# Rotary embedding of the "hg" mixers: from 32 partitions by 1024 columns in place to 128 partitions by 256 columns through gathered copies

## The reference, cut to what matters

```python
z = h @ w_in[l]                       # 256 x 8704: q, f, i, g, then q, k, v of attention, then two gates
qkv = zatt.reshape(B, S, 3, N_GROUPS, ATT_HEADS, ATT_DIM)     # 3 groups, 4 heads, 128 features
for g, (window, dilation) in enumerate(ATT_GROUPS):
    qg = partial_rope(qkv[:, :, 0, g], cos, sin)
    kg = partial_rope(qkv[:, :, 1, g], cos, sin)
    o_g, lse_g = dilated_window_attention(qg, kg, qkv[:, :, 2, g], window, dilation)
# partial_rope: of the 128 features of a head only the first 32 are rotated, as two halves of 16:
#   [r1 * cos - r2 * sin, r2 * cos + r1 * sin, rest unchanged]
```

## Time and profile before

| | |
|---|---|
| runs | 1879.37 us median of 3 (1879.2 to 1879.43) |
| profiled execution | 1879.31 us, of which 1877.5 us lie between its first and last instruction; mean granted clock of TensorE 0.999 |
| TensorE matmul busy | 1863.6 us (99%) |
| VectorE busy | 1265.3 us (67%) |
| ScalarE busy | 944.4 us (50%) |
| GpSimd busy | 62.9 us (3%) |
| DMA | 342.58 MB, mean 182 GB/s |

### The profile page before, as it was taken

One profiled execution on the slowest core, in us unless ns is written; L12 is line 12 of the kernel. 1 busy time (PEld: TensorE's weight loads), 2 busy tenths in 40 slices (PEclk: granted clock), 3 DMA queues, 4 the chain that ended last, 5 costly groups with the idle time before them and its releaser, 6 DMA issues.

```text
span 1877.5 us, 25275 instructions
## 1 busy us (share of the span) xinstructions
PE 1863.6 (99%) x9637; PEld 1586.2 (84%) x9637; DVE 1265.3 (67%) x1559; ACT 944.4 (50%) x1225; POOL 62.9 (3%) x94
## 2 busy tenths in 40 slices
PE   9999999999999999999999999999999999999998
PEld 7888988888888898888889888888889888888886
DVE  4466786466546668745576997677656797776754
ACT  5454574554345446445446545545444645445543
POOL 1010100000000000000000000000000000000000
PEclk9999999999999999999999999999999999999999
DMA  9667545656665665666555554455665554465562
GB/s 327 193 195 218 196 140 193 192 181 186 207 195 183 180 187 145 207 198 184 181 173 185 164 181 143 134 193 186 201 192 174 181 191 159 133 190 170 189 191 79
DMA packets 173656, 342.58 MB, mean 182 GB/s; under 512 B 10992, under 2 KB 11168, under 8 KB 173424
## 3 DMA queue, kind: packets, MB, share of 16 engines
q1 hardware_dynamic: 169376, 327.26, 56.1%
q0 software_dynamic: 4176, 13.90, 2.3%
HBM read 338.49 MB, written 1.05 MB: 181 GB/s over the span
## 4 chain that ended last, share of the span: by engine, by line
PE 88%; DVE 10%; issue 1%; ACT 1%; POOL 0%; POOLq 0%; DVEq 0%; ACTq 0%
PE stream L2365 18%; PE stream L2367 18%; PE stream L2366 18%; PE stream L2560 6%; PE stream L2561 3%; PE aux L2418 3%; DVE wlo L1313 3%; PE stream L2540 3%; PE stream L2541 3%; PE stream L2542 3%; PE stream L2403 2%; PE stream L2394 1%; PE stream L2395 1%; PE stream L2477 1%; PE stream L2479 1%; PE stream L2478 1%
## 5 line engine op out<-in xcount | busy, mean ns | idle before, releaser
L1313 DVE TENSOR_TENSOR wlo<-raw,whi 128x1024 fp32r<-128x1024 f32 x582 | 703.8, 1222 | 472.2 <-ACT whi L786 469.3
L786 ACT ACTIVATE whi<-raw 128x1024 fp32r<-128x1024 f32 x582 | 607.1, 1056 | 543.6 <-PE stream L2367 429.6
L2365 PE MATMUL stream<-whi,x_split 128*128 128x512 f32 x944 | 373.3, 395 | 1.5 <-DVE ak L1324 0.6
L2367 PE MATMUL stream<-whi,x_split 128*128 128x512 f32 x944 | 368.1, 390 | 0.0
L2366 PE MATMUL stream<-wlo,x_split 128*128 128x512 f32 x944 | 367.5, 389 | 0.0
L2365 PE MATMUL stream<-whi,hhi 128*128 128x512 f32 x672 | 263.3, 392 | 0.0
L2367 PE MATMUL stream<-whi,hlo 128*128 128x512 f32 x672 | 261.6, 389 | 0.0
L2366 PE MATMUL stream<-wlo,hhi 128*128 128x512 f32 x672 | 261.5, 389 | 0.0
L2560 PE MATMUL stream<-x_split,whi 128*128 128x512 f32 x672 | 241.4, 398 | 2.8 <-DVE ak L1324 2.1
L2367 PEld LDWEIGHTS stream<-whi,x_split 128*128 128x128 f32 x944 | 177.2, 188 | 37.9
L2365 PEld LDWEIGHTS stream<-whi,x_split 128*128 128x128 f32 x944 | 177.3, 188 | 37.3 <-DVE x_split L1349 1.5
(11 more groups left out here) (345 smaller groups left out, 2105.9 us busy)
## 6 DMA issues: line engine op xcount, KB each, us to landing
raw<-ffn_w_gu SPq DMA_DIRECT2D x175, 512.0 KB, 4.4
raw<-w_in SPq DMA_DIRECT2D x136, 512.0 KB, 4.6
raw<-ffn_w_down SPq DMA_DIRECT2D x88, 512.0 KB, 3.8
raw<-w_up SPq DMA_DIRECT2D x64, 512.0 KB, 4.4
raw<-w_down SPq DMA_DIRECT2D x64, 512.0 KB, 4.3
raw<-c_w_in SPq DMA_DIRECT2D x24, 512.0 KB, 3.9
raw<-ab_w_in SPq DMA_DIRECT2D x20, 512.0 KB, 4.9
raw<-w_out SPq DMA_DIRECT2D x16, 512.0 KB, 3.7
```

Source lines behind the costliest of these rows:

```text
L786: act.activation(split_slots(lin, at, j)[0], raw[:, b % RAW], ACT.Copy).then_inc(hi_ready, 1)
L1313: dve.tensor_tensor(lo, raw[:, b % RAW], hi.bitcast(F32), ALU.subtract).then_inc(lo_ready, 1)
L2365: pe.matmul(bank[tt][:], hi, wh, start=kt == 0, stop=False)
L2367: mm = pe.matmul(bank[tt][:], lo, wh, start=False, stop=kt == last)
```

## The change

The rotation of a chunk no longer works in place. GpSimd gathers the four heads below one another, 32 partitions each, into `rope_own` (the values) and `rope_swap` (the halves exchanged): per chunk eight transfers of 16 partitions by 256 tokens (16 KB) and four of 32 partitions (32 KB). VectorE rotates on 128 partitions by 256 columns. GpSimd then waits for that rotation and issues four transfers of 32 KB that put the rows back into `aq` or `ak`, with a semaphore of their own, `rope_out`; only then does it come to the next chunk. VectorE's rotation moves from the end of loop c (`use`) to the middle of loop c + 1, ahead of block 2's split. ScalarE's exponential of a level moves from the end of loop c to between the splits of blocks 0 and 1 of loop c + 1. TensorE waits for `rope_out` in place of `roped`. The tables of cos and sin are repeated over 128 partitions.

```diff
-    for tag, half, inv, width in (("a", 32, inv_a, P), ("b", 16, inv_b, 32)):
+    for tag, half, inv, width in (("a", 32, inv_a, P), ("b", 16, inv_b, P)):
...
-        rope_swap = [sb(f"rope_swap{i}", [32, 4, S], at=(86 + 4 * i) * KB) for i in range(2)]
+        rope_own = [sb(f"rope_own{i}", [P, S], at=(86 + 2 * i) * KB) for i in range(2)]
+        rope_swap = [sb(f"rope_swap{i}", [P, S], at=(87 + 2 * i) * KB) for i in range(2)]
...
                     pool.wait_ge(evicted, 2 * (st.lins[0].c0 + c - 1) + 2)
-                    if seen.roped >= 2:
-
-                        pool.wait_ge(roped, seen.roped - 1 + seen.rotated)
                     seen.roped += 1
-                    for to, half in ((0, 16), (16, 0)):
-                        pool.dma_start(rope_swap[c % 2][to:to + 16], tiles[half:half + 16]).then_inc(swap_in[c % 2], 16)
+                    for h in range(HEADS_G):
+                        for own, half in ((0, 16), (16, 0)):
+                            to = 32 * h + own
+                            pool.dma_start(rope_swap[c % 2][to:to + 16], tiles[half:half + 16, h]).then_inc(swap_in[c % 2], 16)
+                        pool.dma_start(rope_own[c % 2][32 * h:32 * h + 32], tiles[0:32, h]).then_inc(swap_in[c % 2], 16)
+
+                    pool.wait_ge(roped, seen.roped + seen.rotated)
+                    for h in range(HEADS_G):
+                        pool.dma_start(tiles[0:32, h], rope_own[c % 2][32 * h:32 * h + 32]).then_inc(rope_out, 16)
...
-                    if 3 <= c <= 10:
-                        decay(c - 2)
...
                     def within(c, j):
+                        if lin is into and 4 <= c <= 11 and j == 1:
+                            decay(c - 3)
...
-                    if 5 <= c <= 10:
-                        group = (c - 5) % 3
-                        part = (aq if c < 8 else ak)[0:32, 4 * group:4 * group + 4]
-                        other = rope_swap[c % 2]
-                        seen.swaps += 1
-
-                        dve.wait_ge(swap_in[c % 2], 32 * ((seen.swaps + 1) // 2))
-                        shape = [32, 4, S]
-                        step(dve.tensor_tensor(other[:], other[:], over(cst("sin_b", 32), shape), ALU.mult))
-                        step(dve.tensor_tensor(part, part, over(cst("cos_b", 32), shape), ALU.mult))
-                        dve.tensor_tensor(part, part, other[:], ALU.add).then_inc(roped, 1)
-                        seen.roped += 1
                     if c == 13:
                         head_copies()
+
+                def rotate(c):
+
+                    part, other = rope_own[c % 2], rope_swap[c % 2]
+                    seen.swaps += 1
+
+                    dve.wait_ge(swap_in[c % 2], 192 * ((seen.swaps + 1) // 2))
+                    step(dve.tensor_tensor(other[:], other[:], cst("sin_b"), ALU.mult))
+                    step(dve.tensor_tensor(part[:], part[:], cst("cos_b"), ALU.mult))
+                    dve.tensor_tensor(part[:], part[:], other[:], ALU.add).then_inc(roped, 1)
+                    seen.roped += 1
...
-                layer(into, use, beside(into, -48), lambda c: tiles_from(aq if c < 7 else ak, 4 * ((c - 4) % 3)))
+                later = beside(into, -48)
+
+                def within(c, j):
+                    if 6 <= c <= 11 and j == 2:
+                        rotate(c - 1)
+                    later(c, j)
+
+                layer(into, use, within, lambda c: tiles_from(aq if c < 7 else ak, 4 * ((c - 4) % 3)))
...
-                                pe.wait_ge(roped, r0 + 6)
+                                pe.wait_ge(rope_out, 64 * 6 * (st.layer + 1))
```

More of the change, by code:

```diff
@@ L504, in program @@
         roped = sem("roped")
+        rope_out = sem("rope_out")
         swap_in = [sem(f"swap_in{i}") for i in range(2)]
```

## The result

The changed kernel takes **1904.89 us** in the median of 4 runs (1904.55 to 1906.13), the kernel before 1879.38: a ratio of 1.0138, 95% interval 1.0126 to 1.0150. It is slower by 25.5 us. The traced execution is the slowest of the four (1906.13 us), so differences between the traces add up to 26.8 us and not to 25.5. The prediction had the sign and the place of the loss, but 1890.3 us, and its range ended at 1897.

The account below looks back on a forecast made before the run. TensorE, busy 1863.6 of 1877.5 us, was taken to bound the program, with VectorE full in a mixer's chunks. 1879.31 + 5.6 (waits for put-backs) + 5.4 (clock) = 1890.3 us, range 1878.5 to 1897.

Parts of the forecast that it names:

- VectorE's part: VectorE's rotation per chunk: three operations of 0.42 us, 1.32 us instead of 3.63, load 2.3 us lower.
- The gain that gives: TensorE from chunk 6 to the first logits: 72.2 us instead of 75.05, reached at 1110.8, 2.9 us earlier.
- The moved exponential: ScalarE's exponential in mid-chunk: costs nothing; if its cover went, block 1's split is delayed about 1 us.
- GpSimd's round: GpSimd's gathers, rotation and put-backs in series: one round takes 8.9 + L, 11.7 us.
- L: Time from the last issue to the landing of all transfers: taken as 2.8 us, bounds 2.0 and 3.7.
- Where it ends on the path: TensorE's wait for put-backs at the logits: ends at 1116.5 instead of 1113.7, +2.8 us per layer.
- the rival of the slow transfers: L is 3.7, a round of 12.6 exceeds the chunk, all five count: +6.9 us per layer, 1898.5; chance 0.12.
- The clock: Granted clock falls after TensorE's 5.7 us idle at the logits: 2.7 us per pause, +5.4 in all.
- the rival of the fast transfers: L about 2.1: +0.7 us per layer, the 3.6 us pause costs no clock, 1880.7 us; chance 0.12.

Follow-up runs that it names:

- The run with both cures: Changed kernel with three gathers and one put-back per round and each rotation one VectorE loop earlier: 1874.89 us, ratio 0.9977.
- the spare transfers: Kernel before plus fourteen 16 KB transfers per rotation into a buffer nothing reads: 1882.55 us, ratio 1.0018.

## Why the prediction was right and wrong

- **VectorE's part: right.** The rotation's operations take 0.41 to 0.43 us (predicted 0.42).
- **The gain that gives: right, and not to be had as the change stood.** Predicted were 72.2 us from chunk 6 to the logits in place of 75.05, with the logits at 1110.8. The run with both cures has 1110.77 - 1038.64 = 72.13. The changed kernel itself came there after 73.65 us (1112.37 + 0.89 - 1039.61), since the rounds already held up its later chunks.
- **The moved exponential, priced at nothing: wrong as it stood, right alone.** It costs nothing by itself (1879.28 us); its cover was the rotation that the same change takes away. In the changed kernel VectorE waits 0.9 us per loop for it, and there the old place is 5.9 us better; not by that wait, which is 2.1 us there, but with gathers that land sooner. I had priced the loss of the cover at "about 1 us" and not asked whether the change removes it.
- **GpSimd's round: the form right, L wrong.** 8.9 + L holds: 13.03 measured is L = 4.1. I took 2.8 and an upper bound of 3.7. This is the term that failed. The earlier trace rows give the median of single transfers; a rotation waits for the last of twelve and TensorE for the last of four, so the row's upper part was the one to read, and its 5.6 the bound to keep. The floor of 2.0 was no floor either: single put-backs landed after 1.7 us. The estimate by the Trainium skill (DMA: Bandwidth & Descriptors, Anatomy of one DMA) was 2.04 us; the median landing of the 16 KB gathers is 3.5 us, so the measurement decides against it for transfers beside this stream of weights. The Trainium skill's rule to coalesce under 64 KB (the same page, Rules for kernel authors) is borne out: four transfers in place of sixteen gave 22 us back. (With L = 2.04 my own sum gives 1880.4, not the 1880.6 that I wrote.)
- **Where it ends on the path: the step that fell with L.** I wrote that 8.9 + 2.8 = 11.7 fits into a chunk of 12.1, so that only the last two rounds counted. At L = 4.1 none fits and all five count, as in the rival of the slow transfers, whose working with the measured L gives 50.9 + 5 × 13.0 + 3.0 + 4.1 = 123.0: the logits started at 1123.88. That rival (1898.5 us, 0.12) was the right mechanism at a still too small price. In place of +2.8 us per layer stand 9.2 (10.18 less 0.97) and 9.8 (21.65 less 11.87).
- **The clock: right in kind, 2.7 us for a measured 1.7 and 2.1.** The second logits came 7.85 and 8.31 us after the first instead of 6.16. In the run with four transfers a pause of 2.9 us cost 2.8 and one of 3.0 us 0.1, so the charge neither grows with the pause nor is it sure, and the rival of the fast transfers had no ground to take a pause of 3.6 us as free.
- **A term that was missing: the end of the program**, 3.3 us, which the spare transfers cost by themselves.

Sum in the prediction's form: 9.2 + 9.8 for the waits, 1.7 + 2.1 for the clock, 3.3 for the end and 1.0 from the program's start make 27.1, less 0.3 that TensorE won back behind the second mixer's logits: 26.8, the difference of the spans.

What stays open: why the landings take this long (every run has the stream of weights beside them, so that the stream is the cause is not shown), why the gathers land up to 0.6 us sooner with the exponentials at their old place, when a pause of 3 us brings the clock down and when not, by what rule the end of the program grows, and how the run with the rotation in place in mid-chunk shares its 18 us between the late place and the exponential, which act through each other.

## What to carry to other kernels

A chain of transfer, operation and transfer on an engine that stands in the path of nothing can still set the end: add up its round, with the landing of the *last* transfer of each batch, and compare it with the pace of the loop that it runs beside; if it is longer, every round counts from the first. Before such a chain is made faster, see how early it can begin, and let one transfer carry what sixteen did. And where a change moves two things, ask whether the one was the cover of the other: moving the exponential cost nothing, cost 6 us, or gave back 10 to 13.5, depending on where the rotation stood and what set its rounds.

## What was not expected of the hardware

- The landings beside the weights' stream: the gathers of 16 KB take 1.9 to 4.4 us, median 3.5 (line 731 of the changed kernel by itself, below), those of 64 and 128 KB 3.9 and 4.1 in the median, so eight times the size (16 KB against 128) costs 0.6 us.

```profile
DMA to landing us min/median/max: 1.9/3.5/4.4
```

- Transfers that GpSimd issued long ago cost time at the end of the program: 168 more of 16 KB 3.3 us, and 24 more of 64 and 128 KB in the run with four transfers still 2.0 us. It goes neither by their number alone nor by their size alone.
- A GpSimd product of 32 by 1024 (2.62 us) stretched a VectorE operation from 0.68 to 2.90 us.
- A pause of 2.9 us cost more by its clock (2.8 us) than one of 10.5 us (1.7), and one of 3.0 us in the same execution almost nothing (0.1). Granted clock by stretch, with the pause of 2.9 us from 1110.6 on, then with that of 10.5 from 1113.2 on:

```profile
1113.00:1116.00 3.00, 2.23 (x8) 2.11 (x9) 1.93 (x4) 0.00 (x0) 0.00 (x0) 0.50 0.62 201
1116.00:1119.00 3.00, 3.00 (x8) 2.31 (x7) 0.72 (x2) 1.32 (x3) 0.00 (x0) 0.50 0.04 14
1119.00:1122.00 3.00, 3.00 (x13) 2.49 (x12) 0.61 (x1) 1.06 (x1) 0.00 (x0) 0.88 0.00 0
```

```profile
1116.00:1119.00 3.00, 0.00 (x0) 0.00 (x0) 1.99 (x4) 0.52 (x2) 0.43 (x1) 0.67 0.63 191
1119.00:1122.00 3.00, 0.00 (x0) 0.00 (x0) 2.96 (x6) 0.00 (x0) 1.54 (x4) 0.50 0.51 107
1122.00:1125.00 3.00, 1.12 (x5) 1.15 (x6) 0.56 (x1) 0.00 (x0) 0.00 (x0) 0.50 0.78 287
1125.00:1128.00 3.00, 3.00 (x11) 2.48 (x10) 1.27 (x3) 0.93 (x3) 0.00 (x0) 0.62 0.00 0
1128.00:1131.00 3.00, 3.00 (x15) 2.46 (x14) 0.66 (x1) 1.46 (x2) 0.00 (x0) 1.00 0.00 0
```

Behind the long pause most of the slow stretch (0.50, which is 1.2 GHz) passes while TensorE still idles, and 3.4 us of it while it works; behind the short one TensorE works through nearly 6 us of it, from 1113.8 on.
